# Squares, key transposes and filter transforms of a hybrid attention, Hyena and mixture-of-experts step

## The chip, the cores and the metric

The kernel runs on 1 core of a Trainium2 chip. The metric is the device time of one execution in microseconds (us). A core has TensorE (PE in the profile; PEld is its weight load), VectorE (DVE), ScalarE (ACT), GpSimd (POOL) and SyncE (SP), whose queue issues most of the DMA transfers. The engines run side by side and wait for each other only at semaphores.

## The reference

One layer of a diffusion step for two sequences: 1024 latent tokens and 128 context tokens, model width 1024, all in float32.

```python
h = x * (1 + sc1) + sh1                      # conditioning rows from silu(c) @ w_mod
q, k, v, hy = split(h @ w_in)                # 8 heads, 2 key/value heads of 64; hy: 3 x 512
attn = rms_norm(softmax(q @ k^T / 8) @ v)    # latent tokens also see 128 cached keys
# hyena: implicit filters
h = sin(fr * (sin(fr * (z @ w1 + b1)) @ w2 + b2)) @ w3
h = h * exp(-t * abs(decay))                 # L x 2 directions x 2 orders x 512
g = concat(h[:, 0], 0, reversed h[:, 1])
g = g * rsqrt(sum(g * g) + EPS)              # the squares of the weighed taps
spec = rfft(g)
z = parts[0]
for o in range(2):
    z = parts[o + 1] * (irfft(rfft(z) * spec[o]) + z * skip[o])
x = layer_norm(ALPHA * x + g1 * (concat(attn, rms_norm(z)) @ w_out))
y = layer_norm(ALPHA * x + g2 * experts(x * (1 + sc2) + sh2))   # 32 experts, 2 per token
```

## The kernel before

All the work is one program of five instruction streams, each written out in order. It has these stages.

**Start.** TensorE multiplies the first hidden layer of the filters (`hidden(0)`), eight chunks of the conditioning (`modulation_parts(c)`, `modulation_columns(c)`), of which chunk c needs its 1 MB of `w_mod`, and the second hidden layer (`hidden(1)`, between chunks 2 and 3). VectorE reduces the argument of the sines (L1853 to L1858) and ScalarE takes them (L846).

**Four filter passes.** A pass makes the filters of one order and one half of the channels, as nine tiles of taps (eight latent, one context). For tile j TensorE makes the taps (`taps`), ScalarE the decay window (`window`, L856), VectorE weighs (`weigh_taps`), ScalarE squares (`square`, L863) into one of two buffers `sq`, and GpSimd folds (L650) and adds (L654; L648 for tiles 0 and 8) the squares to `sq_sum`. Then VectorE runs `transform_taps`: sums and differences of the two directions in two groups, the second of which waits for the last square; `odd_differences`; `norm_scales`, which waits for TensorE's `norms`; the odd imaginary tiles; the skip row, which waits for TensorE's `skip_rows`; the odd real tiles; the even tiles. These are the first stages of a Fourier transform over tiles. TensorE finishes it by 22 `spectrum` items in a pass: four of the context, eight odd, ten even. Each is copied from one of two PSUM banks by ScalarE (L871) and stored to DRAM by a DMA from ScalarE's queue, from one of three buffers, so that a copy waits for the store three before.

Between these, TensorE makes 27 tiles of the query, key and value projection (`project_qkv`, eight matmuls of 256 columns each), copied by ScalarE (L879). Its order in passes 1 to 3 is: taps, one tile, the last five spectra of the pass before, norms, two tiles, skip rows, two tiles, the context spectra, the rest of the tiles, the other spectra. In pass 0 it is norms, skip rows, three tiles. ScalarE's queue is in order as well: the last square stands ahead of the copy of the first tile and of the five spectra.

SP's queue waits for `tiles_transformed`, given three times a pass by the transform, and when it has reached 12 it loads the rotary table (`rot`, 0.5 MB), a chunk of `w_in` and one of `w_mod` (1 MB each).

**Then** the Hyena features and tokens (295 to about 500 us), the Hyena convolutions (to 725), attention (to 1000), the output projection and routing (to 1206), the expert loop (to 1594) and the last norm.

**Start of attention.** VectorE splits keys and queries in a high and a low part (`split_keys`, `high_heads`, `low_heads`). TensorE transposes the keys in four blocks of ten tiles (`turn_keys`); each tile is turned twice by a matmul with the identity, into the upper and the lower 64 partitions of PSUM. The eight heads of token tile 0 are turned between blocks 1 and 2. ScalarE copies each block (L995). `scores(0)` waits for all of it, and for each further token tile `scores` and `turn_probs` wait for the semaphore `heads_copied`, given by VectorE.

VectorE has three helpers for a wait between its own instructions: `own` and `give` wait for the instruction just issued, `next_but_one` for the one before it. The filter transforms use `own`, the Hyena transforms `next_but_one`. They record L1626 for every `tensor_tensor`, L1639 for `own` products and L1728 for `next_but_one` products.

```python
            def next_but_one(ins):
                steps[0] += 1
                ins.then_inc(sem("dve_step"), 1)
                dve.wait_ge(sem("dve_step"), steps[0] - 1)
```

## Time and profile before

| | |
|---|---|
| median of 3 runs | 1656.86 us (1655.42 to 1658.33) |
| profiled execution | 1657.55 us, of which the span of instructions is 1655.7 |
| mean granted TensorE clock | 0.949 |
| TensorE busy | 1501.1 us, 91% of the span |
| VectorE busy | 947.7 us, 57% |
| ScalarE, GpSimd busy | 362.8 and 367.4 us, 22% each |

The granted clock is given as a share of full speed: 1.00 is 2.4 GHz and 0.50 is 1.2 GHz. Times in the timeline run from the start of the span. A timeline row merges instructions of one engine and line that follow each other.

### The profile page before, as it was taken

To read this page: it belongs to the slowest core of one execution; us is meant where nothing else is said; L and a number is where in the kernel's file an instruction comes from. 1 tells how busy PE (TensorE), PEld (TensorE's weight loads), DVE (VectorE), ACT (ScalarE), POOL (GpSimd) and SP (SyncE) were. 2 spreads that over 40 slices of the span, in tenths; PEclk is the share of its full clock that TensorE was granted. 3 is DMA by queue.
4 is the path that set the end of the run, shared out by engine and by line. 5 is a ranking of instruction groups with operands and counts; after the bars stand their busy time and mean duration, and the time that the engine had idled before them with its cause. 6 is when DMAs were issued, how large, how long until landed. Compare 5 with 4: busy or idle time off the path is not lost. (4 is left out here: it accounts for less than half of the span.)

```text
span 1655.7 us, 22893 instructions
## 1 busy us (share of the span) xinstructions
PE 1501.1 (91%) x8630; PEld 1086.7 (66%) x8630; DVE 947.7 (57%) x1577; ACT 362.8 (22%) x696; POOL 367.4 (22%) x623
## 2 busy tenths in 40 slices
PE   7689988999998899949999997999489999999985
PEld 3467766444444688848888874455378888888852
DVE  3867876366654999966666653443733333333326
ACT  2553342111110111115655551010000000000004
POOL 0330330011110000000311317746222212222114
PEclk9799998999999999979999997999589999999998
DMA  9422123233321212230000004211458898998845
GB/s 320 148 69 83 44 75 118 67 104 122 122 90 67 90 58 64 70 109 1 2 2 1 2 1 155 74 64 51 165 202 319 338 331 321 332 338 327 306 171 218
DMA packets 102743, 229.27 MB, mean 138 GB/s; under 512 B 12807, under 2 KB 70759, under 8 KB 93896
## 3 DMA queue, kind: packets, MB, share of 16 engines
q1 hardware_dynamic: 78968, 195.86, 33.1%
q0 software_dynamic: 10736, 19.77, 3.4%
q10 hardware_dynamic: 12960, 12.59, 2.3%
q8 instruction: 50, 0.82, 0.2%
q14 instruction: 29, 0.24, 0.0%
HBM read 204.66 MB, written 38.98 MB: 147 GB/s over the span
## 5 line engine op out<-in xcount | busy, mean ns | idle before, releaser
L1110 PE MATMUL PS<-buffer 128*128 128x128 f32 (+7 forms) x5638 | 1255.5, 380 | 90.6 <-DVE buffer L1626 28.1
L1110 PEld LDWEIGHTS PS<-buffer 128*128 128x128 f32 (+2 forms) x5638 | 870.6, 195 | 448.0 <-issue 314.1
L1626 DVE TENSOR_TENSOR buffer<-buffer 128x512 f32<-128x512 f32 (+16 forms) x446 | 258.5, 604 | 26.8 <-ACT buffer L965 11.8
L1626 DVE TENSOR_TENSOR buffer<-PS,buffer 128x512 f32<-128x512 f32 (+2 forms) x143 | 94.4, 690 | 129.6 <-PE PS L1110 116.2
L1113 PE MATMUL PS<-buffer 128*128 128x128 f32 x1136 | 157.0, 280 | 12.7 <-DMA buffer<-moe_inputs,buffer 5.5
L1113 PEld LDWEIGHTS PS<-buffer 128*128 128x128 f32 x1136 | 130.2, 153 | 39.9 <-issue 29.0
L1626 DVE TENSOR_TENSOR buffer<-buffer,PS 128x256 f32<-128x256 f32 (+3 forms) x55 | 27.6, 502 | 205.7 <-PE PS L1110 195.1
L2056 DVE TENSOR_SCALAR_CACHE_REDUCE buffer<-PS 128x1152 f32<-128x1152 f32 (+1 forms) x72 | 89.1, 1238 | 36.4 <-PE PS L1110 35.6
L1004 ACT ACTIVATE buffer<-buffer 128x1152 f32<-128x1152 f32 (+1 forms) x72 | 83.8, 1164 | 107.6 <-DVE buffer L2056 107.5
L1080 ACT ACTIVATE buffer<-PS 128x256 f32<-128x256 f32 x33 | 12.6, 383 | 367.1 <-PE PS L1110 367.1
L2072 DVE COPY buffer<-PS 128x640 f32<-128x640 f32 x64 | 52.8, 825 | 63.1 <-PE PS L1113 62.3
L1443 PE MATMUL PS<-buffer 128*64 128x128 f32 x1168 | 79.3, 279 | 6.1 <-ACT buffer L1037 4.7
L1443 PEld LDWEIGHTS PS<-buffer 128*64 128x64 f32 x1168 | 62.6, 137 | 19.7 <-ACT buffer L1037 13.8
L678 POOL TENSOR_TENSOR buffer<-buffer 128x256 f32<-128x256 f32 (+4 forms) x45 | 17.9, 399 | 258.1 <-ACT buffer L1010 254.7
L1966 DVE TENSOR_SCALAR buffer<-PS,buffer 128x1024 f32<-128x1024 f32 (+1 forms) x24 | 21.0, 877 | 93.8 <-PE PS L1110 93.4
L2257 DVE SCALAR_TENSOR_TENSOR buffer<-PS,buffer 128x1024 f32<-128x1024 f32 x33 | 42.4, 1284 | 40.5 <-PE PS L1110 40.5
L662 POOL TENSOR_TENSOR buffer<-buffer 2x256 f32<-2x256 f32 x16 | 11.9, 746 | 235.4 <-ACT buffer L841 235.4
L1639 DVE SCALAR_TENSOR_TENSOR buffer<-buffer 128x512 f32<-128x512 f32 (+6 forms) x69 | 56.6, 820 | 2.4
L770 POOL COPY buffer<-buffer 128x1 int32 x32 | 5.8, 183 | 232.4 <-DVE buffer L2257 232.4
L2241 DVE COPY buffer<-PS 128x1024 f32<-128x1024 f32 x33 | 40.4, 1225 | 17.6 <-PE PS L1113 17.6
L648 POOL TENSOR_TENSOR buffer<-buffer 128x256 f32<-128x256 f32 x8 | 8.7, 1085 | 168.2 <-ACT buffer L863 168.2
L761 POOL DMA_INDIRECT expert_outputs<-buffer x34 | 34.4, 1012 | 47.1 <-POOL buffer L770 25.5
(170 smaller groups left out, 966.2 us busy)
## 6 DMA issues: line engine op xcount, KB each, us to landing
buffer<-in_exp_w_gate SPq DMA_DIRECT2D x33, 1024.0 KB, 6.8
buffer<-in_exp_w_up SPq DMA_DIRECT2D x33, 1024.0 KB, 9.2
buffer<-in_exp_w_down SPq DMA_DIRECT2D x33, 1024.0 KB, 9.0
buffer<-in_w_mod SPq DMA_DIRECT2D x24, 1024.0 KB, 7.0
filter_spectra<-buffer ACTq DMA_DIRECT2D x88, 128.0 KB, 1.7
buffer<-filter_spectra SPq DMA_DIRECT2D x44, 256.0 KB, 2.6
buffer<-in_w_in SPq DMA_DIRECT2D x9, 1024.0 KB, 5.2
buffer<-expert_outputs SPq DMA_DIRECT2D x4, 1536.0 KB, 17.1
```

The source lines that it names most:

```text
L761: pool.indirect_dma_start(out=y_d[:, :], out_offset=bass.IndirectOffsetOnAxis(ap=rows, axis=0), in_=ybuf[:, s, :], in_offset=None, bounds_ ...
L1004: act.activation(probs[:, i % 2, 0:n], probs[:, i % 2, 0:n], ACT.Exp, bias=nmax[:, i:i + 1], scale=-1.0, accum_out=psums[:, i:i + 1]).then ...
L1110: return nc.tensor.matmul(out, lhsT, rhs, start=start, stop=stop)
L1113: return nc.tensor.transpose(out, in_, ident)
L1443: last = nc.tensor.matmul(PS[HD * u:HD * (u + 1), at:at + P], vals, probsT[:, (first + u) % 4, a, :], start=a == 0, stop=a == len(tiles) - ...
L1626: return dve.tensor_tensor(out, a, b, op)
L1639: own(dve.scalar_tensor_tensor(out, a, s, b, ALU.mult, op))
L1966: own(dve.tensor_scalar(out[:, t0:t1], PS[:, ps0 + t0:ps0 + t1], w[1], w[3], ALU.mult, ALU.add))
L2056: dve.tensor_scalar(probs[:, i % 2, 0:n], PS[:, 0:n], -1.0, None, ALU.mult, ALU.min, accum_out=nmax[:, i:i + 1]).then_inc(sem("max_ready"), 1)
L2072: dve.tensor_copy(probsT[:, i % 4, 4:9, :], PS[:, 2048:2688].rearrange("p (t n) -> p t n", t=5)).then_inc(sem("probsT_d"), 1)
L2241: dve.tensor_copy(xgT[:, s, :, :], PS[:, 0:1024].rearrange("p (k n) -> p k n", k=KT)).then_inc(sem("xT_ready"), 1)
L2257: dve.scalar_tensor_tensor(ybuf[:, s, :], PS[:, 2048:3072], row_scale[:, s, 0:1], row_gain, ALU.mult, ALU.mult).then_inc(sem("y_ready_to_s ...
```

## The change

It has seven parts.

1. `sq` gets a third buffer, laid over `stat` and `logits`, which are used only later; the waits of `square` and of the GpSimd loop follow it.
2. `hidden(1)` stands behind `modulation_columns(0)` on TensorE, ahead of `modulation_parts(2)`.
3. `norms(p)` in passes 1 to 3 moves behind `project_qkv(first + 1)`, and `skip_rows(p)` behind `project_qkv(first + 3)`; in pass 0 tiles 0 and 1 stand between norms and skip rows.
4. `turn_keys` makes one transpose per tile, into partitions 0 to 63. ScalarE copies 64 partitions, and VectorE copies these to partitions 64 to 127 (`double_keys`).
5. `scores(0)` waits for the four doubled blocks. The semaphore `heads_copied` becomes `scores_side_copied`, with four counts more.
6. The filter transforms are written anew: `odd_sums`, `odd_imaginary_tiles`, `odd_real_tiles`, `even_tiles`, with 26 instructions instead of 36, of which several make two tiles at once, and with `next_but_one` for most waits.
7. `odd_sums` holds four products that stood behind `norm_scales` before.

```diff
-        stat = keep.take(3 * 144, "p (a n) -> p a n", a=3)
-        logits = keep.take(NTILE * ROUTE_W, "p (t e) -> p t e", t=NTILE)
+        spare = keep.take(3 * 144 + NTILE * ROUTE_W)
+        stat = spare[:, 0:3 * 144].rearrange("p (a n) -> p a n", a=3)
+        logits = spare[:, 3 * 144:].rearrange("p (t e) -> p t e", t=NTILE)
...
-        sq.append(top.take(HW))
+        sq += [top.take(HW), spare[:, 0:HW]]
...
-                a, b = (sq[n % 2][:, HALF * d:HALF * (d + 1)] for d in range(2))
+                a, b = (sq[n % 3][:, HALF * d:HALF * (d + 1)] for d in range(2))
...
-                if n >= 2:
-                    act.wait_ge(sem("sq_added"), n - 1)
-                act.activation(sq[n % 2], hbuf[:, j, :, :].rearrange("p d c -> p (d c)"), ACT.Square).then_inc(sem("square_ready"), 1)
+                if n >= 3:
+                    act.wait_ge(sem("sq_added"), n - 2)
+                act.activation(sq[n % 3], hbuf[:, j, :, :].rearrange("p d c -> p (d c)"), ACT.Square).then_inc(sem("square_ready"), 1)
...
-                act.copy(kT[:, s, v, :], PS[:, 1536 * (n % 2):1536 * (n % 2) + 10 * P]).then_inc(sem("rows_copied"), 1)
+                act.copy(kT[0:HD, s, v, :], PS[0:HD, 1536 * (n % 2):1536 * (n % 2) + 10 * P]).then_inc(sem("rows_copied"), 1)
...
             modulation_columns(0)
+            hidden(1)
             modulation_parts(2)
             modulation_columns(1)
-            hidden(1)
...
+                    project_qkv(first + 1)
                     norms(p)
-                    project_qkv(first + 1)
                     project_qkv(first + 2)
+                    project_qkv(first + 3)
                     skip_rows(p)
-                    project_qkv(first + 3)
                     project_qkv(first + 4)
                 else:
                     norms(0)
+                    project_qkv(0)
+                    project_qkv(1)
                     skip_rows(0)
-                    for m in range(3):
-                        project_qkv(m)
+                    project_qkv(2)
...
-                    for u in range(2):
-                        last = nc.tensor.matmul(PS[HD * u:HD * (u + 1), at:at + P], k_split[:, s, t, HD * v:HD * (v + 1)].bitcast(F32),
-                                                ident, start=True, stop=True, tile_position=(0, HD * u))
+                    last = turn(PS[0:HD, at:at + P], k_split[:, s, t, HD * v:HD * (v + 1)].bitcast(F32))
...
             pe.wait_ge(sem("rows_copied"), len(KEY_BLOCKS) + 1)
+            pe.wait_ge(sem("scores_side_copied"), len(KEY_BLOCKS))
             scores(0)
...
+            def odd_sums():
+
+                x, w = hbuf[:, 0:NLAT, :, :].rearrange("p j d c -> p j (d c)"), TT_f
+                next_but_one(tt(w[:, 7:10, :], x[:, 1:4, :], x[:, 7:4:-1, :], ALU.subtract))
+                next_but_one(tt(w[:, 2:5, :], x[:, 1:4, :], x[:, 7:4:-1, :], ALU.add))
+                axpy1(w[:, 5, :], w[:, 9, :], C3 / C1, w[:, 7, :])
+                axpy1(w[:, 6, :], w[:, 7, :], C3 / C1, w[:, 9, :], ALU.subtract)
+                axpy1(w[:, 0, :], w[:, 3, :], C2, x[:, 4, :])
+                own(dve.scalar_tensor_tensor(w[:, 1, :], w[:, 3, :], C2, x[:, 4, :], ALU.mult, ALU.subtract))
+
+            def odd_imaginary_tiles():
+
+                a, w = AF_f, TT_f
+                axpy1(a[:, 15, :], w[:, 2, :], C3 / C1, w[:, 4, :])
+                own(dve.scalar_tensor_tensor(a[:, 13, :], w[:, 4, :], -C3 / C1, w[:, 2, :], ALU.mult, ALU.add))
+                own(dve.scalar_tensor_tensor(pair(a, 9, 11), pair(a, 15, 13), -C1, w[:, 0:2, :], ALU.mult, ALU.subtract))
+                next_but_one(dve.scalar_tensor_tensor(pair(a, 15, 13), pair(a, 15, 13), -C1, w[:, 0:2, :], ALU.mult, ALU.add))
+
+            def odd_real_tiles():
+
+                x, a, w = hbuf[:, 0, :, :].rearrange("p d c -> p (d c)"), AF_f, TT_f
+                axpy1(w[:, 0, :], w[:, 8, :], C2, x)
+                own(dve.scalar_tensor_tensor(w[:, 1, :], w[:, 8, :], -C2, x, ALU.mult, ALU.add))
+                axpy1(pair(a, 1, 3), w[:, 5:7, :], C1, w[:, 0:2, :])
+                give(dve.scalar_tensor_tensor(pair(a, 7, 5), w[:, 5:7, :], -C1, w[:, 0:2, :], ALU.mult, ALU.add), "tiles_transformed")
+
+            def even_tiles():
+
+                x, a, w = hbuf[:, 0:NLAT, :, :].rearrange("p j d c -> p j (d c)"), AF_f, TT_f
+                add1(w[:, 0:4, :], x[:, 0:4, :], x[:, 4:8, :])
+                sub1(w[:, 4:8, :], x[:, 0:4, :], x[:, 4:8, :])
+                add1(w[:, 8:10, :], w[:, 0:2, :], w[:, 2:4, :])
...
-                odd_differences(TT_f, lat)
+                odd_sums()
                 norm_scales(p)
...
+            def double_keys(n):
+                v, s = KEY_BLOCKS[n]
+                dve.wait_ge(sem("rows_copied"), n + 1 + (n > 1))
+                dve.tensor_copy(kT[HD:P, s, v, :], kT[0:HD, s, v, :].bitcast(F32)).then_inc(sem("scores_side_copied"), 1)
...
             split_keys(1)
+            for n in range(len(KEY_BLOCKS)):
+                double_keys(n)
```

## Rows read from the trace of the kernel before

**Rows 1.** The page: busy time of each engine

```profile
PE 1501.1 (91%) x8630; PEld 1086.7 (66%) x8630; DVE 947.7 (57%) x1577; ACT 362.8 (22%) x696; POOL 367.4 (22%) x623
```

**Rows 2.** Windows of three stages: length, busy us (instructions) by engine, mean clock, DMA, GB/s

```profile
101.00:161.00 60.00, 55.44 (x219) 40.77 (x218) 46.80 (x68) 22.24 (x48) 14.97 (x16) 0.94 0.22 71
...
740.00:1000.00 260.00, 249.15 (x2401) 209.90 (x2403) 163.53 (x270) 144.36 (x257) 58.60 (x201) 0.99 0.02 4
...
1206.00:1594.00 388.00, 382.76 (x2641) 318.99 (x2642) 134.79 (x133) 13.27 (x34) 83.97 (x165) 0.99 0.83 304
```

**Rows 3.** Timeline of pass 1: start, length, engine, line, instructions, [idle before and releaser]

```profile
112.15 2.03 DVE L1626 TENSOR_TENSOR buffer<-buffer 128x1536 f32<-128x1536 f32 x1
112.52 2.24 POOL L650 TENSOR_TENSOR buffer<-buffer 128x256 f32<-128x256 f32 x1
...
117.05 0.63 ACT L863 ACTIVATE buffer<-buffer 128x512 f32<-128x512 f32 x1 [3.76 <-POOL buffer L654]
...
118.36 23.23 PE L1110 MATMUL PS<-buffer 128*128 128x256 f32 x98 [3.25 <-ACT buffer L871]
118.40 1.44 POOL L648 TENSOR_TENSOR buffer<-buffer 128x256 f32<-128x256 f32 x1
```

**Rows 4.** Windows behind the stalls of passes 1, 2 and 3, columns as in rows 2

```profile
118.36:125.00 6.64, 6.64 (x21) 5.55 (x22) 5.82 (x5) 1.49 (x4) 1.48 (x2) 0.56 0.23 79
178.17:183.00 4.83, 4.83 (x18) 3.96 (x18) 4.73 (x4) 1.40 (x4) 1.49 (x2) 0.65 0.32 108
236.84:241.00 4.16, 4.16 (x12) 3.41 (x13) 4.06 (x4) 1.12 (x3) 2.20 (x3) 0.59 0.30 99
```

**Rows 5.** Timeline of the start, and the DMA view's row of the conditioning weights

```profile
16.67 1.16 ACT L846 ACTIVATE buffer<-buffer 64x1152 f32<-64x1152 f32 x1 [1.27 <-DVE buffer L1858]
...
41.76 0.59 PEld L1139 LDWEIGHTS PS<-buffer 128*32 128x32 f32 x16 [0.76 <-DMA buffer<-in_w_mod]
...
buffer<-in_w_mod SPq DMA_DIRECT2D x8, 1024.0 KB, 12.4
```

**Rows 6.** Timeline of pass 0, TensorE and ScalarE

```profile
57.91 1.84 PE L1110 MATMUL PS<-buffer 128*128 128x1 f32 x8 [9.11 <-POOL buffer L648]
...
65.20 14.56 PE L1110 MATMUL PS<-buffer 128*1 128x128 f32 x60 [5.44 <-DVE buffer L1626]
...
72.02 0.37 ACT L879 COPY buffer<-PS 128x256 f32<-128x256 f32 x1 [10.77 <-PE PS L1110]
...
78.93 0.37 ACT L879 COPY buffer<-PS 128x256 f32<-128x256 f32 x1 [0.96 <-PE PS L1110]
```

**Rows 7.** VectorE in pass 1, grouped by line and shape: count, busy us, mean ns, idle

```profile
L1626 DVE TENSOR_TENSOR buffer<-buffer 128x512 f32<-128x512 f32 x14 | 9.7, 692 | 0.5
...
L1626 DVE TENSOR_TENSOR buffer<-buffer 128x2048 f32<-128x2048 f32 x2 | 4.6, 2292 | 0.1
...
L1635 DVE TENSOR_SCALAR buffer<-buffer 128x512 f32<-128x512 f32 x4 | 1.7, 427 | 0.1
```

**Rows 8.** Timeline of the Hyena stage, VectorE instructions that follow without a gap

```profile
589.31 0.69 DVE L1728 SCALAR_TENSOR_TENSOR buffer<-buffer 128x512 f32<-128x512 f32 x1
589.91 0.69 DVE L1626 TENSOR_TENSOR buffer<-buffer 128x512 f32<-128x512 f32 x1
```

**Rows 9.** Timeline behind the last transform, SP's queue and ScalarE

```profile
273.98 0.33 SPq L468 DMA_DIRECT2D buffer<-in_rot  x1
...
281.30 0.37 ACT L871 COPY buffer<-PS 128x256 f32<-128x256 f32 x1 [3.41 <-DMA filter_spectra<-buffer]
```

**Rows 10.** Timeline of the start of attention, and TensorE transposes at the lower clock

```profile
726.27 7.26 PE L1374 MATMUL PS<-buffer 128*64 128x128 f32 x80 [16.85 <-DVEq L2033]
...
733.46 1.09 PE L1113 MATMUL PS<-buffer 128*128 128x128 f32 x8
...
740.39 1.36 PE L1110 MATMUL PS<-buffer 128*128 128x512 f32 x6 [1.32 <-ACT buffer L995]
...
L1113 PE MATMUL PS<-buffer 128*128 128x128 f32 x8 | 2.0, 428 | 3.2 <-DVE buffer L2116 3.2
```

More of the change, by code:

```diff
@@ L1653, in rsqrt @@
                 own(last) if name is None else give(last, name)
-            def even_tiles(A, W, X, name):
-                own(tt(W[:, 0:4, :], X[:, 0:4, :], X[:, 4:8, :], ALU.add))
-                own(tt(W[:, 4:8, :], X[:, 0:4, :], X[:, 4:8, :], ALU.subtract))
-                w = [W[:, i, :] for i in range(10)]
-                a = [A[:, i, :] for i in range(16)]
-                add(w[8], w[0], w[2])
-                add(w[9], w[1], w[3])
-                add(a[0], w[8], w[9])
-                sub(a[8], w[8], w[9])
-                sub(a[4], w[0], w[2])
-                give(tt(a[12], w[3], w[1], ALU.subtract), name)
-                sub(w[8], w[5], w[7])
-                add(w[9], w[5], w[7])
-                axpy(a[2], w[8], C2, w[4])
-                axpy(a[6], w[8], -C2, w[4])
-                axpy(a[10], w[9], -C2, w[6], ALU.subtract)
-                give(dve.scalar_tensor_tensor(a[14], w[9], -C2, w[6], ALU.mult, ALU.add), name)
@@ L1674, in odd_differences @@
-            def odd_differences(W, X):
-                own(tt(W[:, 0:3, :], X[:, 1:4, :], X[:, 7:4:-1, :], ALU.subtract))
-                own(tt(W[:, 3:6, :], X[:, 1:4, :], X[:, 7:4:-1, :], ALU.add))
-            def odd_real_tiles(A, W, X):
-                w = [W[:, i, :] for i in range(10)]
-                a = [A[:, i, :] for i in range(16)]
-                axpy(w[6], w[1], C2, X[:, 0, :])
-                axpy(w[7], w[1], -C2, X[:, 0, :])
-                scaled(w[8], w[2], C3)
-                axpy(w[8], w[0], C1, w[8])
-                scaled(w[9], w[2], C1)
-                axpy(w[9], w[0], C3, w[9], ALU.subtract)
-                add(a[1], w[6], w[8])
-                sub(a[7], w[6], w[8])
-                add(a[3], w[7], w[9])
-                return tt(a[5], w[7], w[9], ALU.subtract)
@@ L1694, in odd_imaginary_tiles @@
-            def odd_imaginary_tiles(A, W, X):
-                w = [W[:, i, :] for i in range(10)]
-                a = [A[:, i, :] for i in range(16)]
-                axpy(w[6], w[4], C2, X[:, 4, :])
-                axpy(w[7], w[4], C2, X[:, 4, :], ALU.subtract)
-                scaled(w[8], w[5], C1)
-                axpy(w[8], w[3], C3, w[8])
-                scaled(w[9], w[5], C3)
-                axpy(w[9], w[3], C1, w[9], ALU.subtract)
-                axpy(a[9], w[8], -1.0, w[6], ALU.subtract)
-                sub(a[15], w[6], w[8])
-                axpy(a[11], w[9], -1.0, w[7], ALU.subtract)
-                return tt(a[13], w[7], w[9], ALU.subtract)
@@ new lines, in odd_real_tiles @@
+            def odd_real_tiles():
[9 more added lines that the diff above has]
+                add1(w[:, 8:10, :], w[:, 0:2, :], w[:, 2:4, :])
+                sub1(a[:, 4, :], w[:, 0, :], w[:, 2, :])
+                sub1(a[:, 12, :], w[:, 3, :], w[:, 1, :])
+                add1(a[:, 0, :], w[:, 8, :], w[:, 9, :])
+                sub1(a[:, 8, :], w[:, 8, :], w[:, 9, :])
+                sub1(w[:, 0, :], w[:, 5, :], w[:, 7, :])
+                dve.sem_inc(sem("tiles_transformed"), 1)
+                counts["tiles_transformed"] += 1
+                add1(w[:, 1, :], w[:, 5, :], w[:, 7, :])
+                axpy1(a[:, 2, :], w[:, 0, :], C2, w[:, 4, :])
+                axpy1(a[:, 10, :], w[:, 1, :], -C2, w[:, 6, :], ALU.subtract)
+                give(dve.scalar_tensor_tensor(pair(a, 6, 14), w[:, 0:2, :], -C2, pair(w, 4, 6), ALU.mult, ALU.add), "tiles_transformed")
```

13 lines of the change are left out of this document (6 added, 7 removed).

## Prediction

> **What bounds the kernel now.** I read the page's busy times first. TensorE is busy for 91% of the span, VectorE for 57%, the others for 22% [rows 1]. So a saving counts where TensorE waits, or runs at the lower clock. The windows by stage come next: TensorE is busy for 249 of 260 us of attention and 383 of 388 us of the expert loop, so time won ahead of these is kept; but in filter pass 1 it is busy for 55 of 60 us at a mean clock of 0.94 [rows 2].
>
> The timeline of pass 1 shows where [rows 3]. GpSimd sums the squares of the taps. Its adds take 0.73 us alone, but the fold at 112.52 took 2.24: it ended 0.58 us after the VectorE instruction on SBUF of 112.15 + 2.03, and the next add went the same way. ScalarE's last square waited 3.76 us for them (two buffers), and it stands ahead of the copies for which TensorE waits. TensorE stands still for 3.25 us and comes back at 1.2 GHz, half its clock; so it is in passes 2 and 3. The windows behind each stall give the loss, length times (1 - clock): 6.64 x 0.44 = 2.9, 4.83 x 0.35 = 1.7, 4.16 x 0.41 = 1.7, together 6.3 us [rows 4].
>
> **Start.** `hidden(1)` on TensorE moves ahead of `modulation_parts(2)`, which waits for its weights until 18.95. Its input is ready at 17.83 (the sine at 16.67 + 1.16), so it starts 1.1 us before that instead of at about 21.8, the second sine comes up to 4 us earlier, and the parts behind it 2.9 us later. But part 7 waits for the last of the weights at 41.76 anyway [rows 5]: the DMA engines are full until then. The second wait of SP's queue for the parts product comes 3 us later with a backlog of 12 us behind it, so it delays no landing. Windows, squares and sums start earlier: I take 0.5 us (bounds 0 and 2.5, the latter the first weighing 1.4 earlier and one 1.1).
>
> **Third square buffer, passes 1 to 3.** Each of the nine squares may run three ahead. ScalarE then waits only for the add of tile 5 before its last square, so it ends at about 114.6, and the copy that TensorE needs at 115.4 instead of 118.2. The 3.25 us stall becomes 0.4: 2.85 won, three times, 8.6. A gap of 0.4 should leave the clock up: 6.3 more.
>
> What is late next is the sum of squares. I let the engines alternate as in [rows 3], each waiting for the other's instruction (a 256-wide add holds 0.58). VectorE starts 0.9 us earlier (111.3) and no longer pauses, so each of GpSimd's last adds waits for one VectorE instruction: 113.9, 116.1, 117.5, 118.9, 121.1 and, the last, 123.2, against 119.8 now. TensorE reaches `norms` at 115.45 + three spectra (0.86 each, a quarter of a tile's 3.45 [rows 6]) + the one tile now ahead of it = 121.5. It waits 1.7 us, in three passes: -5.1. Behind it are queued the tiles, which only TensorE needs; VectorE wants the norms at 125.7, so it doesn't wait. `skip_rows` behind tile `first+3`, at 131, has its input at 128.8, and VectorE reaches the skip row at 132.4. Bounds of this wait: 0 (sums in time, as now) and 5.5 (GpSimd shut out until VectorE's whole first chain ends).
>
> Here a rule of the Trainium skill bears (SBUF — State Buffer, Who interferes with whom): an instruction of VectorE with two SBUF inputs and a GpSimd instruction that reads SBUF exclude each other for their whole length. It speaks against this change, which lets VectorE run without pauses beside GpSimd. The 2.24 us agree; without the rule (adds of 0.73 throughout) the wait would be nil and the sum 5 us better.
>
> **Pass 0.** Now TensorE waits 9.11 us for the sums (57.91), then 5.44 us for the scaled skip (65.20), and the copy of tile 2 is at 78.93 [rows 6]. By the same alternation the sums end at 59.9, 2.1 later. Then norms 1.84 us, tile 0 with a cold clock 5.2 (between the skip rows at about 66.8 and its copy at 72.02), tile 1 3.45, skip rows 1.0 (their input is ready at 67.0), tile 2 3.45: 74.8 instead of 78.9, 4.1 won. ScalarE's modulation takes 5.7 us from 51.2, done by 57, no wait. Bounds 1.0 (sums at 63) and 6.2 (no delay of them).
>
> **Filter transforms.** 36 VectorE instructions become 26. The trace prices those of 512 columns at 0.69, of 2048 at 2.29 and the scalings at 0.43 [rows 7], each and a gap of 0.03; between the first two a straight line gives 1.23 for 1024 and 1.76 for 1536. Counted from the code, before: 28 x 0.72 + 4 x 0.46 + 2 x 1.79 + 2 x 2.32 = 30.3 us. After: 16 x 0.72 + 6 x 1.26 + the same 8.2 = 27.3. Twenty of them wait only for the last but one: in the Hyena stage such instructions of 0.69 us start every 0.60 [rows 8], 0.12 less, 2.4 in all. So 5.4 us less per pass. TensorE doesn't wait for these tiles (each transform ends before the next taps are made), so in passes 0 to 2 it is worth nothing; the odd sums, now ahead of the norm scales, cost 2.3 us there, hidden as above. Were that cover gone, each pass would gain up to these 5.4.
>
> The Trainium skill says the opposite of the twenty (VectorE: DVE Perf Modes, The DRAIN you can't avoid): leaving out the semaphore saves nothing, only fewer instructions do. The measured start every 0.60 us differs; by the rule the transform would be 3.0 us shorter and the next term 0 instead of 1.5.
>
> **The loads behind the last transform.** Its end releases rot, w_in and w_mod, 2.5 MB. Now they go at 273.98, and three copies of spectra, each of which needs the store three before, wait for it, one for 3.41 us [rows 9]; with the cold clock behind these, pass 3 ends some 8.7 us after the pace of 0.86 would have had it (last copy 294.3, not 285.6). An engine off the path sets this: with the gains so far (0.5 + 4.1 + 4.05 + 2.85 = 11.5) the transform of pass 3 starts at 230.6 - 11.5 - 0.9 = 218.2 and lasts 38.0 (43.3 now, less 1.4 of pause and 5.4, and 1.5 for GpSimd's turns): it ends at 256.2, just when the odd spectra begin (271.0 - 11.5 - 2.9 = 256.6). The first store then takes the 6.4 us that one takes within such a burst (issued 274.8, waited for until 281.3), the fourth copy waits 4.5 us, and the cold clock takes 2.5: 7 us. I take +1.5; bounds -4 (a second round of waits) and +8 (loads done before).
>
> **Attention.** `turn_keys` makes 10 single transposes per block instead of 20 matmuls in halves. Block 0 took 4.6 us cold; a cold transpose is 0.25 (1.98 / 8), a warm one 0.13 (1.09 / 8) [rows 10]: blocks at 2.5, 2.5, then heads and 1.3, 1.3. ScalarE's copies stay 1.23 each, and VectorE adds four doubling copies of 1280 columns, about 0.9 each (2.5 times the 0.43 of 512 columns in [rows 7] is 1.07, and a fixed part doesn't grow), hidden but for the last, on which `scores(0)` now waits as does all of VectorE's softmax behind it. Last block turned 735.4, copied 736.7, doubled 737.6, against scores at 740.39: 2.8 won. Bounds 1.2 (cold to the end, this copy as slow as ScalarE's) and 3.4. The renamed semaphore costs nothing.
>
> **Sum.** 0.5 + 4.1 + (8.6 + 6.3 - 5.1) + 1.5 + 2.8 = 18.7. From the profiled execution's 1657.55 (span 1655.7 and 1.85 around it) 1638.9; it lies 0.7 above the median of the runs. I predict 1639.
>
> **Rivals.**
> - *Sums in time*: GpSimd isn't held longer than now; no norms wait, pass 0 gives 6.2: 1639 - 7 = 1632. For it: the move of the norms by a tile; against: the 2.24 us.
> - *The stall only moves*: norms wait the whole 3.25 us more and the clock falls there: the 9.8 of passes 1 to 3 go, 1649. It is also the time if the half-idle taps alone pull the clock down.
> - *No change*: that, and the burst costs 4 us more with 2 lost in pass 0: 1655 to 1657.
> - *Slower*: GpSimd is shut out until VectorE's first chain ends, sums at 127. Norms wait 5.5 us per pass and the clock is cold behind each for longer (0.8 more): 3 x (2.85 - 5.5 - 0.8) = -10.4 in place of +9.8, pass 0 +1.0: 1639 + 20.2 + 3.1 = 1662. It decides from a wait of about 5.5 us on; for it: VectorE's instructions now follow without a gap; against: in [rows 3] GpSimd got in after each.
>
> **Numbers.** Forecast 0.60 (1634 to 1645), sums in time 0.12, stall moved 0.14, no change 0.08, slower 0.06. So faster by over 0.2% (3.3 us, about what a measurement of this kernel can tell from no change) 0.86, within it 0.08, slower 0.06. The range 1629 to 1651 leaves out the last two, and reaches down to the low case with part of the burst gone.
>
> **What would show it.** After: the last square without its 3.76 us wait; TensorE's gap behind the second spectrum under 1 us at full clock; a new gap of 1 to 2 us ahead of norms; tile 2 copied near 75; transforms of 26 instructions and 29 us; loads of rot going as the odd spectra begin, one copy waiting over 3 us; scores 11 us after the first key transpose instead of 14. The prediction is wrong if norms wait over 4 us, if the clock stays at 0.5 behind the taps, or if the stores wait longer than now.

## The result and the profile after

The changed kernel takes 1644.54 us (median of 4 runs, 1644.07 to 1645.94) against 1656.14 for the kernel before (4 runs, 1655.01 to 1658.33): ratio on record 0.9924, 95% interval 0.9908 to 0.9940 (the quotient of the two medians is 0.9930). The forecast was 1639 with a range of 1629 to 1651. In profiled executions it is 1644.63 against 1657.55: 12.9 us won where 18.7 were forecast. Run once more it took 1643.48 (6 runs, ratio 0.9920, 0.9906 to 0.9935). One run of a1 below took 3063.21 us, far from all others, and is left out of its median and ratio.

The lines of the changed kernel up to the filter transforms stand one higher (TensorE's helper L1111, squares L864, copies of tiles L880). First the page, which answers to [rows 1]: the shares have hardly moved.

```profile
PE 1493.5 (91%) x8510; PEld 1078.5 (66%) x8510; DVE 938.6 (57%) x1541; ACT 360.7 (22%) x696; POOL 379.8 (23%) x623
```

GpSimd is busy for 12 us more, with the same 623 instructions. The timeline of pass 1 shows why, against [rows 3]:

```profile
109.56 2.03 DVE L1627 TENSOR_TENSOR buffer<-buffer 128x1536 f32<-128x1536 f32 x1
110.06 2.12 POOL L655 TENSOR_TENSOR buffer<-buffer 128x256 f32<-128x256 f32 x1
111.63 2.17 DVE L1640 SCALAR_TENSOR_TENSOR buffer<-buffer 128x1536 f32<-128x1536 f32 x1
112.14 2.23 POOL L651 TENSOR_TENSOR buffer<-buffer 128x256 f32<-128x256 f32 x1
112.27 0.63 ACT L864 ACTIVATE buffer<-buffer 128x512 f32<-128x512 f32 x1 [2.25 <-POOL buffer L655]
...
113.58 6.28 PE L1111 MATMUL PS<-buffer 128*128 128x256 f32 x28 [0.33 <-ACT buffer L872]
...
114.45 1.32 POOL L655 TENSOR_TENSOR buffer<-buffer 128x256 f32<-128x256 f32 x1
115.74 1.44 POOL L651 TENSOR_TENSOR buffer<-buffer 128x256 f32<-128x256 f32 x1
117.26 2.12 POOL L655 TENSOR_TENSOR buffer<-buffer 128x256 f32<-128x256 f32 x1
119.34 2.24 POOL L649 TENSOR_TENSOR buffer<-buffer 128x256 f32<-128x256 f32 x1
...
121.63 3.54 PE L1111 MATMUL PS<-buffer 128*128 128x1 f32 x19 [1.77 <-POOL buffer L649]
```

The last square comes 4.8 us earlier, of which 1.8 were won before this pass; it still waits 2.25 us for the add of tile 5, as the forecast had it. TensorE's gap behind the second spectrum is 0.33 us instead of 3.25, and each of GpSimd's last six adds lasts about as long as the instruction of VectorE beside it. So these two engines don't hold each other up at semaphores alone: the adds last two to three times their 0.73 us, with no semaphore inside them. The sums end 12.0 us after VectorE's first sum (the forecast had 11.9), and TensorE waits 1.77 us ahead of `norms` in each of passes 1 to 3. What the forecast didn't have shows in the windows of pass 2, where the norms start at 177.60 (columns as in [rows 2]):

```profile
176.00:178.00 2.00, 0.40 (x4) 0.40 (x4) 2.00 (x2) 0.24 (x1) 1.54 (x1) 1.00 0.00 0
178.00:179.50 1.50, 1.50 (x11) 1.40 (x12) 1.50 (x4) 0.00 (x0) 0.00 (x0) 1.00 0.00 0
179.50:183.00 3.50, 3.50 (x10) 2.79 (x9) 2.95 (x17) 0.00 (x0) 0.00 (x0) 0.51 0.00 0
183.00:185.00 2.00, 2.00 (x11) 1.77 (x10) 1.97 (x3) 0.37 (x1) 0.00 (x0) 1.00 0.00 0
```

Behind the wait the clock falls to 1.2 GHz for 3.5 us, a loss of 1.7. It did so in passes 2 and 3 of this execution, not in pass 1.

Pass 0, against [rows 6]: TensorE waits 11.23 us for the sums (9.11 before). Tiles 0 and 1 now stand where the second wait of 5.44 us was, and it is gone.

```profile
62.14 15.83 PE L1111 MATMUL PS<-buffer 128*128 128x1 f32 x68 [11.23 <-POOL buffer L649]
```

The start, against [rows 5]: VectorE's first sum of pass 0, the first instruction of its filter transform, begins at 52.11, in the kernel before at 50.08. The first two rows are of the changed kernel, SP's queue and VectorE; the next two of the kernel before.

```profile
4.63 3.07 SPq L469 DMA_DIRECT2D buffer<-in_hy_f_w  x1
...
52.11 2.10 DVE L1627 TENSOR_TENSOR buffer<-buffer 128x1536 f32<-128x1536 f32 x1
```

```profile
4.63 1.45 SPq L468 DMA_DIRECT2D buffer<-in_hy_f_w  x1
...
50.08 2.02 DVE L1626 TENSOR_TENSOR buffer<-buffer 128x1536 f32<-128x1536 f32 x1
```

The loads behind the last transform, against [rows 9]: they go as the odd spectra begin, and the fourth copy waits, as forecast.

```profile
263.10 0.33 SPq L469 DMA_DIRECT2D buffer<-in_rot  x1
...
270.26 0.37 ACT L872 COPY buffer<-PS 128x256 f32<-128x256 f32 x1 [4.53 <-DMA filter_spectra<-buffer]
...
283.77 0.37 ACT L872 COPY buffer<-PS 128x256 f32<-128x256 f32 x1 [0.49 <-PE PS L1111]
```

And the start of attention, against [rows 10]: scores come 9.2 us behind the first key transpose, not 14.1. TensorE stands still for 2.35 us ahead of them, where it waited 1.32 us before.

```profile
715.93 6.81 PE L1114 MATMUL PS<-buffer 128*64 128x128 f32 x48 [16.60 <-DVEq L2023]
...
725.10 1.89 PE L1111 MATMUL PS<-buffer 128*128 128x512 f32 x6 [2.35 <-DVE buffer L2039]
```

Read from mark to mark, the two profiles differ so (a copy is ScalarE's; times in brackets are the marks, before and after):

| stage, and the marks | before | after | won | forecast |
|---|---|---|---|---|
| start, to VectorE's first sum of pass 0 | 50.08 | 52.11 | -2.0 | +0.5 |
| pass 0, from there to its last tile's copy (89.55; 87.76) | 39.5 | 35.7 | +3.8 | +4.1 |
| passes 1 to 3, to the copy of the last tile (270.10; 262.77) | 180.55 | 175.01 | +5.5 | +9.8 |
| the last 18 spectra (294.29; 283.77) | 24.2 | 21.0 | +3.2 | +1.5 |
| to the first key transpose (726.27; 715.93) | 432.0 | 432.2 | -0.2 | 0 |
| attention, to the 16 matmuls of L1460 near its end (982.24; 969.05) | 256.0 | 253.1 | +2.9 | +2.8 |
| the rest | | | -0.3 | 0 |

So two terms are short of the forecast: the start by 2.5 and passes 1 to 3 by 4.3. The experiments ask for the cause of both, and whether the other terms are what they seem.

### The profile page after: what moved, and what is told of

Read it like the earlier page. It is cut to its first block and busy times, and to the rows that moved or that the text cites. A ratio compares the mean times of both kernels' runs of the same rounds, so it can differ in the third digit from the quotient of the medians.

```text
span 1642.8 us, 22621 instructions
## 1 busy us (share of the span) xinstructions
PE 1493.5 (91%) x8510; PEld 1078.5 (66%) x8510; DVE 938.6 (57%) x1541; ACT 360.7 (22%) x696; POOL 379.8 (23%) x623
## 5 line engine op out<-in xcount | busy, mean ns | idle before, releaser
L1111 PE MATMUL PS<-buffer 128*128 128x128 f32 (+6 forms) x5638 | 1253.4, 379 | 84.1 <-DVE buffer L1627 22.4
L1111 PEld LDWEIGHTS PS<-buffer 128*128 128x128 f32 (+2 forms) x5638 | 867.7, 195 | 442.1 <-issue 309.1
L1627 DVE TENSOR_TENSOR buffer<-buffer 128x256 f32<-128x256 f32 (+16 forms) x418 | 240.5, 605 | 19.1 <-ACT buffer L966 11.8
L1114 PE MATMUL PS<-buffer 128*128 128x128 f32 (+1 forms) x1176 | 163.6, 283 | 29.0 <-DVEq L2023 16.6
L1114 PEld LDWEIGHTS PS<-buffer 128*128 128x128 f32 (+1 forms) x1176 | 136.3, 153 | 57.1 <-issue 28.0
L1443 PEld LDWEIGHTS PS<-buffer 128*64 128x64 f32 x1168 | 62.6, 137 | 19.7 <-ACT buffer L1038 13.8
L1675 DVE SCALAR_TENSOR_TENSOR buffer<-buffer 128x512 f32<-128x512 f32 (+1 forms) x120 | 68.6, 614 | 0.4
L663 POOL TENSOR_TENSOR buffer<-buffer 2x256 f32<-2x256 f32 x16 | 11.9, 747 | 227.8 <-ACT buffer L842 227.8
## 6 DMA issues: line engine op xcount, KB each, us to landing
buffer<-filter_spectra SPq DMA_DIRECT2D x44, 256.0 KB, 2.6
```

Of the source, the lines that this page charges most:

```text
L1111: return nc.tensor.matmul(out, lhsT, rhs, start=start, stop=stop)
L1114: return nc.tensor.transpose(out, in_, ident)
L1443: last = nc.tensor.matmul(PS[HD * u:HD * (u + 1), at:at + P], vals, probsT[:, (first + u) % 4, a, :], start=a == 0, stop=a == len(tiles) - ...
L1627: return dve.tensor_tensor(out, a, b, op)
L1675: next_but_one(dve.scalar_tensor_tensor(out, a, s, b, ALU.mult, op))
```

## The experiments

Each median is of 4 to 6 runs, beside 11 of the kernel before on the same chip (a1 to a4, a5 to a8 and a9 to a12 share theirs; each of these three groups ran on another chip, so that medians of different groups are best compared by what each won over its own kernel before). "Start" is VectorE's first sum of pass 0 in the profile, "passes" the time from the copy of the last tile of pass 0 to that of pass 3.

| run | median us | before | ratio (95% interval) | start | passes |
|---|---|---|---|---|---|
| a1 hidden(1) back | 1646.10 | 1657.41 | 0.9921 (0.9904-0.9939) | 55.07 | 176.8 |
| a2 two buffers | 1646.02 | 1657.41 | 0.9930 (0.9913-0.9947) | 49.46 | 178.8 |
| a3 old transforms | 1644.81 | 1657.41 | 0.9916 (0.9901-0.9931) | 49.65 | 176.7 |
| a4 old keys | 1647.09 | 1657.41 | 0.9929 (0.9909-0.9948) | 52.58 | 176.7 |
| a5 norms back | 1666.02 | 1658.22 | 1.0047 (1.0033-1.0060) | 51.59 | 190.5 |
| a6 norms later | 1633.48 | 1658.22 | 0.9846 (0.9832-0.9860) | 49.77 | 166.5 |
| a7 split | 1632.84 | 1658.22 | 0.9850 (0.9833-0.9868) | 52.05 | 166.2 |
| a8 loads behind | 1642.61 | 1658.22 | 0.9902 (0.9886-0.9918) | 50.45 | 176.7 |
| a9 split, loads | 1628.02 | 1657.03 | 0.9825 (0.9808-0.9842) | 52.39 | 166.2 |
| a10 tile ahead | 1627.93 | 1657.03 | 0.9829 (0.9815-0.9844) | 51.10 | 166.3 |
| a11 split, two buffers | 1636.27 | 1657.03 | 0.9878 (0.9863-0.9893) | 51.55 | 169.4 |
| a12 changed again | 1643.48 | 1657.03 | 0.9920 (0.9906-0.9935) | 50.07 | 176.7 |

**a1, the old place of hidden(1).**

```diff
-            hidden(1)
             modulation_parts(2)
             modulation_columns(1)
+            hidden(1)
```

> The changed kernel with hidden(1) back in its old place, all else kept. In the changed kernel's profile the first weighing chain ended at 52.11 us against 50.08 before, 2.0 us late, and 2.5 short of the forecast. Theory 1, the move did not cause it: the issue of the third kind of load took 3.07 us instead of 1.45 and the loads moved 185 GB/s instead of 347 at 16 to 18 us, before hidden(1) could act at 19.9; then the time stays at 1644.5 within 1.5 us, and the chain ends anywhere from 50 to 52.5. Theory 2, the move holds back SP's wait for the parts product (26.17 against 21.97) and with it the last weights: then about 1642.3, 2.0 to 2.5 less, and part 7 starts at 41.8 instead of 43.9.

1646.10 us: no measurable difference, and its passes (176.8 us) and attention (254.2) are those of the repeat a12 (176.7, 254.0). Its profile starts later than any other (55.07). So neither the 2.0 us late start nor any gain of the move can be read from one profile. With the new place, twelve profiles have the first sum at 49.5 to 52.6, mean 51.1, and where the issue of `in_hy_f_w` took only 1.4 to 1.5 us it stands at 49.65 (a3), 49.77 (a6) and 50.07 (a12), against 50.08 in the kernel before with 1.45. The old place with a slow issue (2.51) gave 55.07; the new place with 2.48 to 2.65 gave 51.6 to 52.6 (a7, a11, a4). That hints that the move wins 0 to 0.4 us in a quick start and some 3 (2.5 to 3.5) in a slow one, with only one profile of the old place for each. Shown is that the start of the changed kernel differs by 2.0 us between two executions (52.11 and 50.07), and by 3.1 over the twelve profiles that share this order, later for the most part where the issue is longer.

**a2, two buffers.**

```diff
-                a, b = (sq[n % 3][:, HALF * d:HALF * (d + 1)] for d in range(2))
+                a, b = (sq[n % 2][:, HALF * d:HALF * (d + 1)] for d in range(2))
...
-                if n >= 3:
-                    act.wait_ge(sem("sq_added"), n - 2)
-                act.activation(sq[n % 3], hbuf[:, j, :, :].rearrange("p d c -> p (d c)"), ACT.Square).then_inc(sem("square_ready"), 1)
+                if n >= 2:
+                    act.wait_ge(sem("sq_added"), n - 1)
+                act.activation(sq[n % 2], hbuf[:, j, :, :].rearrange("p d c -> p (d c)"), ACT.Square).then_inc(sem("square_ready"), 1)
```

> The changed kernel with two buffers for the squares instead of three. Theory 1, the third buffer is what took the 3.25 us stall away and costs the new wait ahead of the norms: the last square waits 3.5 us or more again, TensorE stands still for 3 us behind the second spectrum in passes 1 to 3 and the clock falls there, 6.3 us in all; in exchange the norms wait (1.77 us now, a clock loss of 1.7 in two passes) shrinks to nothing. So 3 x 2.9 + 6.3 - 3 x 1.77 - 3.4 = 6.3 us more, 1651. Rival, the stall only moved (what was won behind the spectrum was given back ahead of the norms): within 2 us of 1644.5.

1646.02, not 1651. The stall is back and the wait ahead of norms is gone, both as theory 1 has it:

```profile
112.63 0.63 ACT L864 ACTIVATE buffer<-buffer 128x512 f32<-128x512 f32 x1 [3.76 <-POOL buffer L655]
...
113.93 2.40 PE L1111 MATMUL PS<-buffer 128*128 128x256 f32 x10 [3.25 <-ACT buffer L872]
```

But the passes take only 2.1 us more (178.8 against 176.7). The stretch behind the stall, from the copy of the pass's first tile to that of its second, takes 7.09 us in pass 1, 8.59 in pass 2, 10.07 in pass 3, and 7.08 in a11 at full clock: the clock took 0, 1.5 and 3.0 us, 4.5 together and not 6.3. The expectation had added the clock lost in one profile of before as if it were the same each time. The rival is nearer than theory 1: of what the third buffer wins, most is given back ahead of the norms.

**a3, the old transforms.** The edit puts back the old filter transforms with their 36 instructions, in the old order.

> The changed kernel with the old filter transforms of 36 instructions. Theory 1, as forecast: worth nothing in passes 0 to 2, since each transform ends before the next taps; in pass 3 the loads go out later by 5 us and collide elsewhere, so the burst costs between 4 less and 3 more: 1641 to 1648, with the transform at 43 us instead of 38 and TensorE's waits in passes 1 and 2 unchanged. Rival: the shorter transform carries part of the gain in each pass: 1649 to 1660, with new waits of TensorE for tiles_transformed.

1644.81, and the passes take 176.7 us as in a1, a4 and a12, so the shorter transform is worth nothing in passes 0 to 2. From VectorE's first sum to its last instruction in pass 1 it takes 44.65 us (107.83 to 152.48) against 37.93 (109.56 to 147.49). Of the 6.7, 2.05 are a wait for the norms that the new order hides:

```profile
121.30 0.16 DVE L1887 TENSOR_SCALAR buffer<-PS 128x4 f32<-128x4 f32 x1 [2.05 <-PE PS L1111]
...
124.27 1.42 DVE L1640 SCALAR_TENSOR_TENSOR buffer<-buffer 128x512 f32<-128x512 f32 x2
125.72 0.43 DVE L1636 TENSOR_SCALAR buffer<-buffer 128x512 f32<-128x512 f32 x1
```

The loads of pass 3 go at 267.87 instead of 263.10; the last 18 spectra take 21.6 us against 21.0. The median is the changed kernel's within the spread, as forecast.

**a4, the old key transposes.**

```diff
-                    last = turn(PS[0:HD, at:at + P], k_split[:, s, t, HD * v:HD * (v + 1)].bitcast(F32))
+                    for u in range(2):
+                        last = nc.tensor.matmul(PS[HD * u:HD * (u + 1), at:at + P], k_split[:, s, t, HD * v:HD * (v + 1)].bitcast(F32),
+                                                ident, start=True, stop=True, tile_position=(0, HD * u))
...
```

ScalarE copies 128 partitions again, and `double_keys` with its waits is left out.

> The changed kernel with the old key transposes in halves of 64 rows and no doubling copies. Theory 1: the 2.85 us that the attention stage won (10.34 ahead at its start, 13.19 at its end) are theirs: 1647.4, and scores start 14.1 us after the first key transpose instead of 9.2. Rival: scores won 4.95 us and lost 2.1 again at the cold clock behind them, so the rows of before would give it all back: 1649.5 where the clock is warm sooner in the old order; or 1644.5 if the attention's pace is set by VectorE's later work.

1647.09, which the time alone doesn't tell from a1 to a3 (1644.8 to 1646.1). From the first key transpose to the mark at the end of attention it takes 255.7 us (718.70 to 974.39), before 256.0, with the new transposes 253.1 (changed kernel), 254.2 (a1) and 254.0 (a12), and between these in a2, a3, a6, a8 and a11 too. So they win 1.5 to 2.6 us: theory 1 holds, at the low side of the 2.85.

These profiles show what the new order costs as well. The second group of six matmuls of scores takes 2.39 to 2.40 us in all twelve profiles with the new transposes, behind a stop of 2.3 to 2.4 us for the last doubled block ahead of the first group; it takes 1.37 in the kernel before and in a4, where that stop is 1.32. In the changed kernel the clock is 0.50 from 726 to 732.

**a5, norms in their old places.** The third part of the change undone: norms one tile earlier in passes 1 to 3, and pass 0 in the old order.

```diff
+                    norms(p)
                     project_qkv(first + 1)
-                    norms(p)
                     project_qkv(first + 2)
+                    skip_rows(p)
                     project_qkv(first + 3)
-                    skip_rows(p)
...
```

> The changed kernel with norms and skip_rows in their old places among the in-projection tiles, in pass 0 too. The runs so far start up to 3 us apart before anything that was changed (tile 0 of pass 0 is copied anywhere from 66.4 to 73.1 us), so stages are read from copy to copy: passes 1 to 3 from the last tile of one to that of the next, 175.0 to 176.8 us with the change, 180.6 before. Theory 1: TensorE reaches the norms a tile (3.45 us) sooner and waits 5.2 us for GpSimd's sums in each pass, so passes 1 to 3 take 186 us or more, and the time is 1655 or more: the third buffer without this move would win nothing. Rival: the sums come when they come because VectorE and GpSimd share the time, and the wait then is the same 1.8: 1645.

1666.02, slower than the kernel before. TensorE waits 5.21 us for the sums in each of passes 1 to 3, and in pass 1 the clock stays at half for some 7 us behind it:

```profile
126.25 8.97 PE L1111 MATMUL PS<-buffer 128*128 128x1 f32 x28 [5.21 <-POOL buffer L649]
```

```profile
128.00:130.00 2.00, 2.00 (x6) 1.64 (x7) 1.72 (x9) 0.00 (x0) 0.00 (x0) 0.50 0.00 0
130.00:132.00 2.00, 2.00 (x7) 1.55 (x6) 1.73 (x9) 0.00 (x0) 0.00 (x0) 0.50 0.00 0
```

The passes take 13.8 us more, pass 0 another 5.2 (40.8 against 35.7), the last spectra 1.8. So the new place of the norms, in pass 0 and in the others, is what makes the change a gain: with all the rest and without it the kernel is 0.5% slower than before. How much the third buffer alone does without this move was not run.

**a6, norms one tile later still.**

```diff
                     project_qkv(first + 1)
-                    norms(p)
                     project_qkv(first + 2)
+                    norms(p)
                     project_qkv(first + 3)
```

> The changed kernel with norms(p) of passes 1 to 3 one more tile later, behind tile first+2. Theory 1 (the sums' wait of 1.77 us is real and the cold clock behind it, 0 to 3.4 us and mostly 1.7 in the five profiles, hangs on it): no wait, full clock, passes 1 to 3 at 175.0 - 3 x 1.77 - 3.4 = 166.3 us plus nothing, time 1636 to 1638. VectorE waits about 1.5 us for the norms, which costs nothing. Rival 1: skip_rows, now one tile behind, waits for the scaled skip instead and the clock falls there: 175 again. Rival 2: the clock falls behind norms whatever goes ahead: 169.7.

1633.48, below the 1636 to 1638 expected, in part because the expectation started from passes of 175.0 where the mean is 176.4. In pass 1 TensorE has no wait from the second spectrum to the last of the five tiles and the clock stays at 1.00, VectorE waits 0.27 us for the norms, and the passes take 166.5 us. That is 9.9 less than in the six profiles that keep this wait, 1.77 us three times each (changed kernel, a1, a3, a4, a8, a12; from 175.0 to 176.8, mean 176.4). 5.3 of it are the waits, and the 4.6 left are the clock behind them. So the norms themselves don't bring the lower clock (rival 2), the wait ahead of them does. The copy-to-copy times of the tiles on both sides of these 18 waits are 6.39 us in 3 cases, 8.05 to 8.07 in 13 and 9.74 in 2: losses of 0, 1.7 and 3.4, mean 1.6. They are not spread evenly over the passes: in pass 3 it is 1.7 in all six profiles, and 0 and 3.4 come in passes 1 and 2 only. Here are the windows of one of the last (a12, pass 1, norms at 120.09):

```profile
119.00:121.00 2.00, 0.91 (x6) 0.91 (x7) 2.00 (x3) 0.00 (x0) 1.04 (x1) 0.87 0.00 0
121.00:123.00 2.00, 2.00 (x7) 1.73 (x8) 1.89 (x6) 0.00 (x0) 0.00 (x0) 0.50 0.00 0
123.00:125.00 2.00, 2.00 (x6) 1.60 (x5) 1.64 (x10) 0.00 (x0) 0.00 (x0) 0.50 0.00 0
125.00:127.00 2.00, 2.00 (x6) 1.59 (x5) 1.89 (x5) 0.00 (x0) 0.00 (x0) 0.50 0.00 0
```

**a7, VectorE's first pairs split.**

```diff
-                for j0, j1 in ((0, 6), (6, NTILE)):
+                for j0, j1 in ((0, 3), (3, 6), (6, NTILE)):
```

> The changed kernel with VectorE's first pair of instructions of each filter transform (six tiles each) split into two pairs of three tiles. Theory 1, each of GpSimd's adds waits for one instruction of VectorE, whatever its length: the adds behind the instructions of three tiles took 1.32 to 1.44 us in the profile, those behind six tiles 2.12 to 2.24, so the sums end at about 118.2 instead of 121.6 and TensorE, there at 119.9, doesn't wait: passes 1 to 3 at 166.5 us; in pass 0 the sums come 3 us sooner, of which the modulation lets 1 to 2 through: 1634 to 1637. Rival, GpSimd's adds are slow for as long as VectorE is busy, by a share and not by turns: the adds keep their pace, sums as late as now, 1644.5.

1632.84, with passes of 166.2 us. GpSimd's adds go down to what three tiles cost:

```profile
107.02 1.23 DVE L1627 TENSOR_TENSOR buffer<-buffer 128x768 f32<-128x768 f32 x1
107.51 1.32 POOL L655 TENSOR_TENSOR buffer<-buffer 128x256 f32<-128x256 f32 x1
108.28 1.37 DVE L1640 SCALAR_TENSOR_TENSOR buffer<-buffer 128x768 f32<-128x768 f32 x1
108.79 1.44 POOL L651 TENSOR_TENSOR buffer<-buffer 128x256 f32<-128x256 f32 x1
...
114.40 1.44 POOL L649 TENSOR_TENSOR buffer<-buffer 128x256 f32<-128x256 f32 x1
115.28 3.83 DVE L1627 TENSOR_TENSOR buffer<-buffer 128x1536 f32<-128x1536 f32 x2
```

The sums end 8.8 us after VectorE's first sum instead of 12.0, and TensorE has no wait for them in passes 1 to 3. So GpSimd waits by instruction of VectorE, not by share of its time: the rival is out. Pass 0 takes 33.2 us, and 34.5 in a9 where it is the same, against 35.7 in the changed kernel and 36.2 in its repeat.

**a8 and a9, the loads of 2.5 MB.** a8 adds one wait, the second of the three new lines; a9 is a7 with all three, so that `w_mod` goes ahead of `rot` and `w_in`, and its load and its wait in the old place are left out.

```diff
             sp.wait_ge(sem("tiles_transformed"), 3 * PASSES)
+            sp.wait_ge(sem("taps_ready"), PASSES * NTILE)
+            sp.wait_ge(sem("spectrum_copied"), PASSES * N_SPEC - 1)
+            load_w_mod(COND_CHUNKS)
             load(rot, I["rot"], "gains_loaded")
...
```

> The changed kernel with rot, w_in and w_mod sent only when all but the last spectrum of pass 3 are copied, and not at the end of the last transform. Theory 1: the stores of spectra are held up by these 2.5 MB; without them the spectra keep 0.83 to 0.86 us each, and the stretch from the last tile's copy to the last spectrum's takes 15.5 us and not 21.0: 1639. The loads (some 6.7 us) are down by 285, before the parts that need them at 285.7. Rival: the feature stage then waits for w_mod or w_in as long as the stores did: 1644.5, the stretch shorter and the next one longer by the same.

> The split version with the loads of rot, w_in and w_mod behind all but the last spectrum's copy, and w_mod, which TensorE needs first, sent first of the three. Sending them late with rot and w_in ahead won 5.6 us among the stores and gave 4.0 back: 2.2 of waiting for w_mod and the cold clock behind it. Theory 1, the order of the three decides: 1 MB of w_mod is down some 3 us after its issue, long before TensorE asks 9 us later, so all 5.6 us stay: 1632.8 - 5.6 = 1627. Rival: what comes last of the three is then late in its turn (rot or w_in), 1631 or more.

In a8 the last 18 spectra take 15.4 us instead of 21.0, as expected: the loads cost 5.6 there. But `w_mod` is late, the clock falls behind the wait (0.50 from 291 to 293), and the stretch to the first key transpose takes 436.1 instead of 432.2; 1642.61 is 1 to 2 below the changed kernel. In a9 the 15.4 stay and the next stretch takes 431.9: 1628.02, 1 us from the 1627 of theory 1. The first row is of a8, the two below it of a9:

```profile
289.33 1.40 PE L1141 MATMUL PS<-buffer 128*32 128x256 f32 x16 [2.18 <-DMA buffer<-in_w_mod]
```

```profile
268.11 0.55 SPq L469 DMA_DIRECT2D buffer<-in_w_mod  x1
...
275.99 1.07 PE L1141 MATMUL PS<-buffer 128*32 128x256 f32 x16
```

**a10, tile 0 ahead of norms(0)**, on top of a9.

```diff
-                    norms(0)
                     project_qkv(0)
+                    norms(0)
                     project_qkv(1)
```

> The version before this one, with tile 0 of pass 0 ahead of norms(0) instead of behind it. In the split version TensorE waits 8.82 us for the sums, until 59.67, and tile 0's modulated input is there at 58.9. Theory 1: tile 0 fills the wait, norms start near 63 and are still there when VectorE wants them at 66, and the copy of tile 2 comes 1 to 2 us sooner relative to the end of the weighing (22.5 us in the split version): 1626. Rival 1: VectorE sets pass 0 (its transform ends at 89.7 and the even spectra need it): no change, 1627. Rival 2: norms come too late for VectorE and its whole chain shifts: 1628 to 1630.

1627.93 against 1628.02 for a9: no difference that can be measured. In the profiles pass 0 takes 32.6 us against 34.5 (a9) and 33.2 (a7). Inconclusive: pass 0 is the same in a9 and a7 and still differs by 1.4 us, so a gain of 1 to 2 us can't be read from one profile.

**a11, split with two buffers**: the edit of a2 on top of a7.

> The split version with two buffers for the squares. In the changed kernel, going back to two buffers cost about 2 us in the stages (178.8 against 176.7 us in passes 1 to 3), since the 1.77 us wait ahead of the norms went when the 3.25 us stall came back. With VectorE's pairs split there is no such wait to give back. Theory 1: the last square waits for two adds of 1.4 instead of 2.2 us each, 2.2 us instead of 3.76; TensorE stands still for some 1.7 us in each of passes 1 to 3, and the clock falls behind about two of these waits: passes 1 to 3 at 166.2 + 5.1 + 3.4 = 174.7, 1641. Rival: with short instructions the sums are fast enough for two buffers as well: 1633, and the third buffer is needed only because the instructions are long.

1636.27, 3.4 above a7 (4.6 by what each won over its own kernel before). The stall behind the second spectrum is 1.65, 1.29 and 1.65 us, and 169.4 - 166.2 = 3.2 us is all it costs: the clock stays up behind all three. The rival is out, and theory 1 had the wait right and the clock wrong again, this time too dear. Beside the split the third buffer is worth 3 to 5 us, not the 8 expected.

**a12, the changed kernel again**, without an edit.

> The changed kernel once more, for its spread and its start. In the profiles so far the clock fell behind a 1.77 us wait ahead of the norms by 0 to 3.4 us, and tile 0 of pass 0 was copied anywhere from 66.4 to 73.1. Theory 1 (the start is not the kernel's doing, and the clock behind each wait is drawn anew in each execution): the start differs from the 2.0 us late of the first profile by 1 us or more, passes 1 to 3 take 173 to 177 us, the time is 1643 to 1646. Rival: both are the kernel's: the weighing ends at 52.1 again, and the waits of passes 2 and 3 are followed by the cold clock and that of pass 1 isn't, 175.0.

1643.48. The start is at 50.07 instead of 52.11, and the clock losses behind the norms' waits are 3.4, 0 and 1.7 instead of 0, 1.7 and 1.7. So theory 1 holds for the start and for passes 1 and 2; in pass 3 the loss was the same in every profile.

## Why the prediction came out 5.5 us too low

The likeliest case was right in most of its mechanisms, and 1644.5 lies in the wide range and, by half a microsecond, in its own (1634 to 1645). What it leaves out, in two places, is what the clock costs behind a new stop of TensorE. Step by step:

- **Start, forecast +0.5, profile -2.0.** Neither shown nor refuted: the start moved by 2.0 us between two executions of the changed kernel, the second of which lies at 50.07 as the kernel before does (50.08), and a1 took no more time than its spread allows. The step took a single profile as the price of the loads.
- **Pass 0, +4.1, measured +3.8.** Right in mechanism; the size is a little flattered by this profile. The seven profiles with this pass 0 (changed kernel, a1, a3, a4, a6, a8, a12) take 35.7 to 37.1 us, mean 36.3, so it is 3.1 in the mean against the one profile of before (39.5). The sums ended 9.9 us after the first sum (forecast 9.8).
- **Stall behind the spectrum, "3.25 becomes 0.4".** 0.33; right, with "a gap of 0.4 should leave the clock up".
- **"It waits 1.7 us, in three passes: -5.1".** The wait was 1.77 every time, and this is the step that failed: it priced the wait and not the clock behind it, though [rows 4] show what a stop of 3.25 us brings. The rival *the stall only moves* named this clock, but only together with a wait of 3.25. Measured (18 waits) it is 1.6 us each, 4.7 in a kernel; a6 and a7 take away wait and clock together and shorten the passes by 9.9 and 10.2. With it the term of passes 1 to 3 is 9.8 - 4.7 = 5.1; the profile had 5.5, since in it one of the three waits cost no clock, and the mean of six profiles is 180.55 - 176.4 = 4.1.
- **GpSimd and VectorE in turns.** Right to 0.1 us, and a7 shows it by its length. The Trainium skill (SBUF — State Buffer, Who interferes with whom) says that a VectorE instruction with two SBUF inputs contends with a GpSimd instruction that reads SBUF, and that this is an exclusive lock; the traces agree for GpSimd, with 1.32 to 1.44 us beside three tiles and 2.12 to 2.24 beside six, for an add of 0.73.
- **Transforms, 5.4 us less, worth nothing in passes 0 to 2.** Worth nothing: right (a3). The transform of pass 1 takes 37.9 us, and the forecast had 38.0 for that of pass 3. Against a3 it is 6.7 - 2.05 = 4.7 less work; that the 0.7 to the forecast's 5.4 went to GpSimd's turns is likely and not shown. Instructions of 512 columns that wait for the last but one start every 0.60 us (two from 145.07 to 146.28), those of a3 that wait for the last one every 0.73 (two from 124.27 to 125.72). The Trainium skill (VectorE: DVE Perf Modes, The DRAIN you can't avoid) says that leaving out the semaphore saves nothing, and in the same section that a next instruction that is not held starts earlier. Here waiting one instruction later saves 0.12 us each, so for these instructions the first of the two doesn't hold.
- **The loads, +1.5, measured +3.2.** The time within the pass (263.10, just ahead of the first odd spectrum's copy at 263.64), the place and the 4.5 us wait were right; the loss is 21.0 - 15.4 = 5.6, not 7: the clock was low for 3.5 us (about 1.7 lost), not for 5.
- **Attention, +2.8, measured +2.9** in the profile, 1.5 to 2.6 by a4 and the repeats. That the profile agrees is luck. Scores came 9.2 us behind the first transpose, 2.1 sooner than forecast, since the clock was 1.00 again at 719 and the second block was turned in 1.4 us and not in 2.5. But the forecast had TensorE stand still from 735.4 to 737.6 for the last doubled block and put the clock behind this stop at nothing, as ahead of the norms: it stood still for 2.35 us, and the scores ran at the lower clock (2.39 us for the second six matmuls against 1.37 before). The two misses cancel.

So 18.7 becomes 12.9: passes -4.3, start -2.5, loads +1.7, pass 0 -0.3, attention +0.1, and -0.5 in the stretches that the change doesn't touch. The first two are partly chance, since the start and the clock losses differ between executions. What stays open: why the clock falls behind one wait of 1.77 us and not behind the next, and what hidden(1) is worth.

The best version here is a9 (or a10): 1628.0 us, 29 below the kernel before. By what each won over its own kernel before, the change gives 12 to 14, the split of two VectorE instructions 12 to 14 and the place and order of three loads about 4.

## What to carry to other kernels

A buffer more moves the wait to the next thing that is late; look for it before, and move TensorE's work with it, or the change makes the kernel slower (a5). Price each stop of TensorE with the clock behind it, as a mean over several profiles where there are any. Where two engines shut each other out instruction by instruction, cut the long instructions of the one that can spare it: the other's queue shortens by as much; and a large load that is released by an engine off the path wants a place and an order chosen by who needs it first.

## What the runs showed of the hardware that was not expected

- The clock behind equal waits at an equal place differs from execution to execution: behind 1.77 us ahead of `norms` it took 0, 1.7 or 3.4 us (3, 13 and 2 of 18), behind 3.25 us in a2 0, 1.5 and 3.0, behind 1.3 to 1.65 us in a11 nothing in three cases. Of the 18, the six of pass 3 all lost 1.7. What TensorE does around the wait differs too: in the first case matmuls of one column follow it.
- A stop of 2.3 to 2.4 us ahead of the first scores was followed by the lower clock in twelve of twelve profiles, one of 1.32 us at the same place in none of two.
- Splitting an instruction of 1536 columns (2.03 and 2.17 us) into two of 768 cost VectorE nothing in the end: the four take 1.1 us more (1.23 to 1.37 each, with GpSimd's turns in them), but the whole transform of pass 1 took 37.96 us in a7 (107.02 to 144.98) against 37.93. GpSimd was done earlier, and the next two of 1536 columns took 3.83 us instead of 4.37.
- The issue of one small load at 4.63 us took 1.4 to 3.1 us in different executions, and the first sum of pass 0 came between 49.5 and 52.6, mostly later where the issue was longer. That the issue is the cause is not shown. So one profile says nothing on a start shifted by less than 3 us.
